# Prompt attention with undivided probabilities: the reciprocal sums spread by a product, the value products one step later

## What is computed

```python
s = jnp.einsum('bqhc,bkc->bhqk', ql, ckv_p) + jnp.einsum('bqhr,bkr->bhqk', qr, kr_p)
s = s.astype(jnp.float32) * MLA_SCALE
s = jnp.where(k_idx[None, :] <= q_idx[:, None], s, -jnp.inf)
p = jax.nn.softmax(s, axis=-1).astype(ckv_p.dtype)
return jnp.einsum('bhqk,bkc->bqhc', p, ckv_p)
```

## Time and profile before

| | us |
|---|---|
| median of 3 runs | 2792.64 |
| lowest and highest of them | 2786.09, 2794.36 |
| the profiled execution | 2795.52 |
| its span in the trace | 2793.7 |
| prompt attention stage in it, about | 150.6 to 352.7 |

### The profile page before, as it was taken

One profiled execution on the slowest core, in us unless ns is written; L12 is line 12 of the kernel. 1 busy time (PEld: TensorE's weight loads), 2 busy tenths in 40 slices (PEclk: granted clock), 3 DMA queues, 4 the chain that ended last, 5 costly groups with the idle time before them and its releaser, 6 DMA issues. The chain is left out here.

```text
span 2793.7 us, 36499 instructions
## 1 busy us (share of the span) xinstructions
PE 2474.0 (89%) x13126; PEld 1851.2 (66%) x13126; DVE 1362.5 (49%) x2701; ACT 1044.8 (37%) x1662; POOL 579.3 (21%) x452
## 2 busy tenths in 40 slices
PE   8888888899966679999998669999999999999990
PEld 4455556564455646666454448999989999989990
DVE  0545544200066601011266137777777777777764
ACT  1145533200023100000021026666666766666652
POOL 0020022000000000000035103344433444344423
PEclk9989989999999889999999889999999999999995
DMA  3000043210010040100113069999999999999964
GB/s 131 0 12 1 1 154 151 87 38 0 0 41 0 0 170 23 45 23 23 51 31 112 15 233 271 287 282 285 287 285 285 298 287 287 273 292 281 284 176 155
DMA packets 113752, 395.23 MB, mean 141 GB/s; under 512 B 41590, under 2 KB 50886, under 8 KB 85254
## 3 DMA queue, kind: packets, MB, share of 16 engines
q1 hardware_dynamic: 78390, 269.63, 27.3%
q0 software_dynamic: 35296, 124.70, 18.1%
HBM read 325.74 MB, written 69.13 MB: 141 GB/s over the span
## 5 line engine op out<-in xcount | busy, mean ns | idle before, releaser
L1934 PE MATMUL banks<-split 128*128 128x384 f32 x1792 | 538.2, 363 | 0.0
L2048 DVE TENSOR_TENSOR split<-rest,split 128x2048 fp32r<-128x2048 f32 x192 | 438.8, 2286 | 108.2 <-ACT split L1992 91.4
L1932 PE MATMUL banks<-split 128*128 128x192 f32 x2048 | 482.7, 256 | 0.0
L1954 PE MATMUL banks<-split 128*128 128x512 f32 x1536 | 406.8, 407 | 17.3 <-ACT rest L2005 14.6
L1932 PEld LDWEIGHTS banks<-split 128*128 128x128 f32 x2048 | 389.1, 192 | 2.7
L1992 ACT CAST split<-rest 128x2048 fp32r<-128x2048 f32 x192 | 359.3, 1904 | 65.0 <-DMA rest<-in_w_exp_gate 60.1
L1393 PE MATMUL banks<-big 128*128 128x368 f32 x1152 | 358.9, 475 | 14.5 <-DMA big<-in_w_merge 14.5
L1934 PEld LDWEIGHTS banks<-split 128*128 128x128 f32 x1792 | 338.9, 189 | 0.0
L1882 POOL DMA_INDIRECT y_rows<-rest x128 | 266.7, 2083 | 336.5 <-ACT rest L2005 299.0
L1954 PEld LDWEIGHTS banks<-split 128*128 128x128 f32 x1536 | 276.5, 190 | 71.9 <-ACT rest L2005 17.5
L1393 PEld LDWEIGHTS banks<-big 128*128 128x128 f32 x1152 | 220.0, 191 | 153.1 <-issue 17.0
(11 more groups left out here) (327 smaller groups left out, 3088.0 us busy)
## 6 DMA issues: line engine op xcount, KB each, us to landing
rest<-in_w_exp_gate SPq DMA_DIRECT2D x64, 1024.0 KB, 9.1
rest<-in_w_exp_up SPq DMA_DIRECT2D x64, 1024.0 KB
rest<-in_w_exp_down SPq DMA_DIRECT2D x64, 1024.0 KB, 7.1
big<-in_w_merge SPq DMA_DIRECT2D x8, 1536.0 KB, 6.3
big<-in_w_cols SPq DMA_DIRECT2D x11, 512.0 KB, 3.8
x_rows<-big SPq DMA_DIRECT2D x9, 512.0 KB
y_rows<-big SPq DMA_DIRECT2D x9, 512.0 KB, 2.6
big<-in_x_cols SPq DMA_DIRECT2D x3, 1472.0 KB, 17.7
```

What stands on the lines that cost most here:

```text
L1932: ins = pe.matmul(PS[:, banks[f], 0:CAP], wr[:, s, j, LO, at:at + 128], x[:, k, 0:2], start=False, stop=False)
L1934: ins = pe.matmul(PS[:, banks[f], 0:2 * CAP], wr[:, s, j, HI, at:at + 128], x[:, k], start=False, stop=(k == KD - 1))
L1954: ins = pe.matmul(PS[:, DBANK[c]], hr[:, a, f, HALF * hf:HALF * hf + 128], wr[:, s, DOWN, b, at:at + 512], start=(f == 0 and j == 0), stop ...
L2048: dve.tensor_tensor(wr[:, s, j, LO], raw[:, s, j], wr[:, s, j, HI].bitcast(F32), ALU.subtract).then_inc(parted[j], 1)
```

## The change

```diff
-    s_full, max_ready, exp_done, p_ready = sem("a_s"), sem("a_max"), sem("a_e"), sem("a_p")
+    s_full, max_ready, exp_done, rinv_ready, diag_ready = sem("a_s"), sem("a_max"), sem("a_e"), sem("a_ri"), sem("a_dg")
...
+    eye_ready, diag = sem("a_eye"), arena.take(4, 128)
+    ones, factor = arena.take(VDIM), arena.take(2, 128)
...
-    for step in range(2, U + 2):
+    for step in range(2, U + 4):
+        if step >= 5 and step % 2:
+            unit(("f", (step - 5) // 2), "A")
...
         own = Steps(pool, picked)
+        for w in range(U):
+            pool.wait_ge(rinv_ready, w + 1)
+            if w >= 4:
+                pool.wait_ge(o_full, (w - 4) // 2 + 1)
+            pool.tensor_scalar(diag[:, w % 4], S.ident, sums[:, w:w + 1], None, ALU.mult).then_inc(diag_ready, 1)
         for p in range(4):
...
         def turn_probs(w):
-            pe.wait_ge(p_ready, w + 1)
+            pe.wait_ge(exp_done, w + 1)
...
+        def factors(m):
+            name = ("f", m)
+            pe.wait_ge(diag_ready, 2 * m + 2)
+            await_bank(pe, name)
+            for e in range(2):
+                ins = pe.matmul(PS[VDIM * e:VDIM * (e + 1), bank(name), 0:128], ones, diag[:, (2 * m + e) % 4], start=True, stop=True)
+            ins.then_inc(staged, 1)
...
-            if step >= 4 and step % 2 == 0:
-                values(step // 2 - 2)
+            if step >= 5 and step % 2:
+                factors((step - 5) // 2)
+                values((step - 5) // 2)
...
-            if step >= 4 and step % 2 == 0:
-                m = step // 2 - 2
-                p, i, _ = UNITS[2 * m]
-                act.wait_ge(o_full, m + 1)
-                act.copy(S.mlaT[:, p, 128 * i:128 * (i + 1)], PS[:, 6, 0:128]).then_inc(o_copied, 1)
+            if step >= 5 and step % 2:
+                m = (step - 5) // 2
+                act.wait_ge(staged, number[("f", m)] + 1)
+                if m >= 2:
+                    act.wait_ge(o_copied, m - 1)
+                act.copy(factor[:, m % 2], PS[:, bank(("f", m)), 0:128]).then_inc(copied_act, 1)
...
-        def normalise(w):
+        def invert(w):
             dve.wait_ge(exp_done, w + 1)
-            own.link(dve.reciprocal(sums[:, w:w + 1], sums[:, w:w + 1]))
-            dve.tensor_scalar(probs[:, w % 4, 0:span(w)], probs[:, w % 4, 0:span(w)], sums[:, w:w + 1], None, ALU.mult).then_inc(p_ready, 1)
-
+            dve.reciprocal(sums[:, w:w + 1], sums[:, w:w + 1]).then_inc(rinv_ready, 1)
+
+        def take_out(m):
+            p, i, _ = UNITS[2 * m]
+            dve.wait_ge(o_full, m + 1)
+            await_copy(dve, ("f", m))
+            dve.tensor_tensor(S.mlaT[:, p, 128 * i:128 * (i + 1)], PS[:, 6, 0:128], factor[:, m % 2], ALU.mult).then_inc(o_copied, 1)
+
+        dve.memset(ones, 1.0).then_inc(eye_ready, 1)
...
             if 1 <= step < U + 1:
-                normalise(step - 1)
+                invert(step - 1)
...
+            if step >= 5 and step % 2:
+                take_out((step - 5) // 2)
```

More of the change, by code:

```diff
@@ L317, in stage_prompt_attention @@
     setup, bf_ready, kr_ready, kv_out = sem("a_setup"), sem("a_bf"), sem("a_kr"), sem("a_out")
-    s_full, max_ready, exp_done, p_ready = sem("a_s"), sem("a_max"), sem("a_e"), sem("a_p")
+    s_full, max_ready, exp_done, rinv_ready, diag_ready = sem("a_s"), sem("a_max"), sem("a_e"), sem("a_ri"), sem("a_dg")
     staged, copied_act, copied_dve = sem("a_st"), sem("a_cpa"), sem("a_cpd")
-    o_full, o_copied, own_s, picked = sem("a_of"), sem("a_oc"), sem("a_own"), sem("a_pick")
+    eye_ready, diag = sem("a_eye"), arena.take(4, 128)
+    ones, factor = arena.take(VDIM), arena.take(2, 128)
+    o_full, o_copied, picked = sem("a_of"), sem("a_oc"), sem("a_pick")
     K = NOPE + ROPE
@@ L343, in stage_prompt_attention @@
         unit(("v", i), "DA"[i % 2])
-    for step in range(2, U + 2):
+    for step in range(2, U + 4):
+        if step >= 5 and step % 2:
+            unit(("f", (step - 5) // 2), "A")
+        if step >= U + 2:
+            continue
         w = step - 2
@@ L463, in values @@
             ins.then_inc(o_full, 1)
+        def factors(m):
[5 more added lines that the diff above has]
+            ins.then_inc(staged, 1)
         for c in range(2):
             keys(0, c)
+        pe.wait_ge(eye_ready, 1)
         for step in range(U + 4):
@@ L526, in _ @@
     def _(dve):
-        own = Steps(dve, own_s)
-        def normalise(w):
+        def invert(w):
             dve.wait_ge(exp_done, w + 1)
-            own.link(dve.reciprocal(sums[:, w:w + 1], sums[:, w:w + 1]))
-            dve.tensor_scalar(probs[:, w % 4, 0:span(w)], probs[:, w % 4, 0:span(w)], sums[:, w:w + 1], None, ALU.mult).then_inc(p_ready, 1)
+            dve.reciprocal(sums[:, w:w + 1], sums[:, w:w + 1]).then_inc(rinv_ready, 1)
[5 more added lines that the diff above has]
+        dve.memset(ones, 1.0).then_inc(eye_ready, 1)
         dve.tensor_copy(S.ident_b, S.ident).then_inc(bf_ready, 1)
@@ L537, in _ @@
         dve.tensor_copy(causal_b, causal).then_inc(bf_ready, 1)
-        for step in range(U + 2):
+        for step in range(U + 4):
             if step < U:
```

## The result

The changed kernel takes 2760.22 us (median of 4 runs, 2758.05 to 2766.79) against 2791.56 of the kernel before in the same comparison: a ratio of 0.990, 95% interval 0.9877 to 0.9923, 31 us less. The forecast was 2776 (2764 to 2788): the direction was right, and the time lies 4 us under the range. The profiled execution has a span of 2756.5 us, where the one before had 2793.7.

A forecast was written before the change was run, and what follows sets the result against it. PE was taken as the bound, idle 31.5 us before the value products. 25.4 us saved up to the last exponentials, less 8.5 at the stage's end, gave -17 us: 2776 us against the median 2792.64, range 2764 to 2788.

The forecast's parts named there:

- Behind the barrier everything is as it was: Stages after the changed one, which start at a barrier: only shifted in time, otherwise unchanged.
- What bounds the kernel, and what goes: PE waits 31.5 us before the value products for ACT's copies; all before the last scores go, -28.9 us.
- New waits (+3): Allowance for new waits in the stream, on factor copies and staging banks: +3 us, bounds 0 and +10.
- The bank without margin: Second half of block 7's transposes needs the factor's bank, free at about 2.9 us, just when PE arrives.
- The -1: Waits on normalised probabilities, 1.4 us in the window: about 1 us goes.
- The clock (-5): PE's granted clock in the stage, 0.96 with four dips: dips go with the waits, -5 us, bounds 0 and -7.
- Product with ones (+7.3): 32 pairs of small products on PE at 0.25 us, 29 before the last scores: +7.3 us, to +12.8.
- Diagonals, `take_out`, factor copy: Per-operation times taken: POOL's diagonal 0.4 us, DVE's `take_out` 0.3, ACT's factor copy 0.27.
- The end (+8.5): End of the stage: POOL's 12.6 us of picks now run behind the 64th diagonal, before the barrier; +8.5 us.
- The slower one: Copies' waits come back at the transposes (L457), nothing of the 28.9 goes: +14, 2807 us; chance 0.05.
- the one in which half of the waits comes back: Waits of 0.4 us per pair, 13 us instead of 3, from a ring through DVE, ACT, PE: 2786; chance 0.15.
- The clock as it was: Rival: PE's clock in the stage stays unchanged: -12 us, 2781, within the forecast's range; no separate chance given.

The follow-up runs named there:

- the picks last: Kernel before with POOL's 49 picks held until the last unit's probabilities are normalised, nothing else changed: median 15.6 us above the kernel before, ratio 1.0036 to 1.0069.
- undivided probabilities alone: Changed kernel with products with ones, value products, factor copy and `take_out` back on the even steps: +0.6 us against the kernel before, ratio 0.9984 to 1.0012.
- the runs with the picks moved to either side: Changed kernel with picks ahead of the diagonals: -32.9, -36.2, -27.0 us against the kernel before; kernel before with picks last: +15.6 us.
- the second comparison: Repeat on one chip against the kernel before: changed -24.5 us, changed with picks first -36.2, kernel before with only value products and their copy one step later -32.4.
- the other two comparisons of variants: Timings against the kernel before of order only (-42.1, -36.9 us), picks first (-32.9, -27.0), undivided only (+0.6), no factor (-40.7), changed (-20.4), picks last (+15.6).

## Why the prediction was right or wrong

**The step that failed.** 31.3 us were gained where 17 were forecast, and that put the time under the range. 5.1 of the 14 us lie in the stage, where the mechanism was right and several terms were mis-sized: the allowance for new waits and the clock above all. The other 9 lie outside the stage, for which the prediction put exactly nothing ("Behind the barrier everything is as it was"). The lower end of the range had 22 us for the stage, which is what the stage then gained (22.0), and 6.5 us for scatter; the first comparison had 9 more than the stage. Of the same two kernels two repeats gave 24.5 and 20.4 us, which from 2791.56 would be 2767 and 2771, inside the range. What made up the 9 us is open.

**What bounds the kernel, and what goes: right.** The waits before the value products are gone, 28.9 us of them up to the last scores, and the order did it. A fell by 30.7 us (195.9 to 165.2), by 30.2 between the means of three traces each (before twice and with the picks last; changed). Forecast: 25.4. Of the 30.7 us 29.5 are of the steady part; 1.3 are of the opening, which the change leaves nearly as it was and which goes by the clock.

**New waits (+3): too dear, about 1.** The ring of exponentials, factor copy, `take_out` and maximum is there (DVE waits 30.6 us in it) and PE never feels it. The bank without margin cost 0.17 us, three times in the stretch shown. I had worked out a margin of 0.6 us before the value products and none at one bank, and then put 3 us on top that no row asked for. In the steady part the idle time of PE fell from 29.1 to 0.9 us, by 28.2, where the three terms on waits (-28.9, -1, +3) make 26.9. The -1 was a misreading: its row is one of weight loads (PEld), and PE stayed busy over them.

**The clock (-5): somewhat too small.** The granted clock was 0.96 in the steady part of both traces of the kernel before, with four dips to the lower level (1.2 GHz); 0.04 of 169 us is some 7 us. It was 0.93 in the kernel with the picks last, 1.00 in all ten traces without the waits, and 0.98 with two dips with undivided probabilities alone, where 18 waits stay. By the 1.4 us of a dip above, an estimate for four is 5.6 us; so what came back is between 5.6 and 7. "TensorE: Matmul & The Clock Gate" of the Trainium skill, Part 1 (The HAM clock gate), says that activity releases the throttle. These traces agree: with PE busy throughout, the clock was 1.00. I had shaded the rule for rows that did not contradict it.

**Product with ones (+7.3): nearly right.** 6.8 us measured in the steady part. The three corrections so far (1.3 for waits, 0.6 to 2 for the clock, 0.5 here) leave 0.3 to 1.7 of the 4.1 us by which the steady part gained more than forecast without a name.

**Diagonals, `take_out`, factor copy: right in kind.** 0.60 us on POOL (0.4 taken, bounds 0.3 and 2.46), 0.29 on DVE (0.3), 0.26 on ACT (0.27). None lies on PE's path. The late library load is not to be seen: POOL waited 12.2 us for the first reciprocal anyway.

**The end (+8.5): right.** B rose by 8.7 us, and the runs with the picks moved to either side give 8.8 to 9.0 and 8.4. With the steady part 4.1 better, the opening 1.3 shorter and the end 0.2 to 0.3 dearer, the stage gained 5.1 us more than forecast.

**"Behind the barrier everything is as it was": not refuted in kind, failed in the number.** The first comparison had 9 us beyond the stage. Of two repeats one has 4 (24.5 for 20.3) and one 2 less than the stage (20.4 for 22.3), and the sample stage, which seemed to carry 6.5 us of it, took 161 to 168 in traces of one and the same kernel. What was forecast as an exact zero came out as anything from -9 to +7 us beside the stage. I had allowed for it only by the 6.5 us of the runs shown, and all of them were of one kernel in one place. Why two medians of different programs differ by more than their stages explain is not settled.

**The rivals.** None came. The slower one, and the one in which half of the waits comes back, stood on a ring that turned out to have room. The clock as it was: refuted.

## What to carry to other kernels

When the fullest engine idles for the last link of a chain that began with its own latest work, look first for independent work to put between, by one step of the order; here two moved lines were worth more than the whole rewrite. Then look at what an edit appends to a stage that ends at a barrier: 12.6 us of copies that nobody needed before the next stage cost 9 us only by their place. Once the fullest engine is busy throughout, relieving an idle engine by adding to the full one is a loss; here it cost 6 us.

## What the runs showed of the hardware

PE's granted clock went with gaps of 1 to 2.4 us that have much work around them. In the steady part it was 0.93 to 0.96 with 18 such gaps, of which none was longer than 2.40 us, and 1.00 in the ten traces whose longest gap was 0.31 us. Each dip to 1.2 GHz cost some 1.4 us.

In five of the fourteen traces ACT and DVE stop, mostly both, for 2 to 10 us with no instruction that could have released them, and the waits are put down as remote. Some of these stops are in the sample stage while the indirect loads fill the DMA engines (share 0.97 and more); others, of 8.5 to 10 us on ACT, are in the routing stage, where that share is 0.02 to 0.04. So a full DMA is not their cause in general. They are in all four traces of the second comparison and in none of the eight of the other two comparisons of variants, which ran on other chips: they go with the chip or the time, not with the kernel. In the first trace of the kernel before, and in the second of the changed one:

```profile
376.88 0.59 ACT L830 COPY big<-banks 128x512 f32<-128x512 f32 x1 [6.33 <-remote]
```

```profile
ACT big L859 <- remote: 5.7, 1, 5.7
```

The changed kernel's first trace has none and the shorter sample stage; its third has none either and the longest, 168.2. So they are not what sets that stage's length, and what does stays open.
